# Seven quarter products for eight in the left half of nine down blocks of each feed-forward stage

## The reference

```python
def _swiglu(h, w_gu, w_down):
    g, u = jnp.split(h @ w_gu, 2, axis=-1)
    return (jax.nn.silu(g) * u) @ w_down

x = x + 0.5 * _rmsnorm(_swiglu(_rmsnorm(x, ffn1_pre_g), ffn1_w_gu, ffn1_w_down), ffn1_post_g)
```

## Time and profile before

| | |
|---|---|
| median of 3 runs | 1080.8 us (1080.31 to 1081.05) |
| profiled execution: time | 1081.31 us |
| profiled execution: span, first to last instruction | 1079.4 us |
| mean granted TensorE clock | 1.000 |
| PE busy | 1068.7 us, 99% of the span |
| DVE busy | 789.1 us, 73% |
| ACT busy | 608.5 us, 56% |

### The profile page before, as it was taken

How to read it: one execution, slowest core, us unless ns; L and a number is a source line. 1 busy time by engine, 2 the same in 40 slices (tenths; PEclk the granted TensorE clock), 3 DMA queues, 4 the chain that set the end, 5 groups by cost and what they waited for, 6 DMA issues and landing times.

```text
span 1079.4 us, 21082 instructions
## 1 busy us (share of the span) xinstructions
PE 1068.7 (99%) x8534; PEld 1009.7 (94%) x8534; DVE 789.1 (73%) x1125; ACT 608.5 (56%) x905; POOL 0.2 (0%) x4
## 2 busy tenths in 40 slices
PE   9999999999999999999999999999999999999999
PEld 7999999999989999999999998999999799999898
DVE  5665556989979777778778555775655887997884
ACT  5544444678586545878445556444444575655471
POOL 0000000000000000000000000000000000000000
PEclk9999999999999999999999999999999999999999
DMA  9866556465543454444546533465556355542251
GB/s 343 292 213 211 176 182 209 151 221 174 179 154 121 152 181 157 157 164 149 208 166 244 196 106 130 147 230 198 188 182 212 119 177 200 191 157 95 102 196 39
DMA packets 29297, 190.71 MB, mean 177 GB/s; under 512 B 3656, under 2 KB 4521, under 8 KB 7466
## 3 DMA queue, kind: packets, MB, share of 16 engines
...
HBM read 188.62 MB, written 1.05 MB: 176 GB/s over the span
## 4 chain that ended last, share of the span: by engine, by line
PE 87%; DVE 9%; ACT 2%; issue 1%; DMA 1%; SPq 0%; DVEq 0%; ACTq 0%
PE bank L526 15%; PE bank L528 15%; PE bank L527 15%; PE bank L538 10%; PE bank L539 10%; PE bank L540 10%; DVE sb_w_lo L2098 3%; PE bank L625 2%; PE bank L761 1%; DVE sb_ssd_conv L2409 1%; DMA sb_w_raw<-in_w 1%; PE bank L709 1%; PE bank L886 1%; ACT sb_w_hi L1371 1%; PE bank L1048 1%
## 5 line engine op out<-in xcount | busy, mean ns | idle before, releaser
L2098 DVE TENSOR_TENSOR sb_w_lo<-sb_w_raw,sb_w_hi 128x2048 fp32r<-128x2048 f32 x169 | 386.4, 2289 | 118.9 <-ACT sb_w_hi L1371 118.5
L1371 ACT ACTIVATE sb_w_hi<-sb_w_raw 128x2048 fp32r<-128x2048 f32 x169 | 322.9, 1911 | 33.0 <-PE bank L528 29.2
L526 PE MATMUL bank<-sb_hT_hi,sb_w_hi 128*128 128x256 f32 (+1 forms) x816 | 225.7, 277 | 0.0
L528 PE MATMUL bank<-sb_hT_hi,sb_w_lo 128*128 128x256 f32 (+1 forms) x816 | 225.7, 277 | 0.0
L527 PE MATMUL bank<-sb_hT_lo,sb_w_hi 128*128 128x256 f32 (+1 forms) x816 | 225.6, 276 | 0.0
L538 PE MATMUL bank<-sb_hT_hi,sb_w_hi 128*128 128x256 f32 (+2 forms) x744 | 213.1, 286 | 0.2 <-DVE sb_hT_lo L2175 0.2
L539 PE MATMUL bank<-sb_hT_lo,sb_w_hi 128*128 128x256 f32 (+2 forms) x744 | 206.2, 277 | 0.0
L540 PE MATMUL bank<-sb_hT_hi,sb_w_lo 128*128 128x256 f32 x744 | 205.9, 277 | 0.0
L526 PEld LDWEIGHTS bank<-sb_hT_hi,sb_w_hi 128*128 128x128 f32 (+1 forms) x816 | 152.7, 187 | 0.0
L528 PEld LDWEIGHTS bank<-sb_hT_hi,sb_w_lo 128*128 128x128 f32 (+1 forms) x816 | 152.6, 187 | 0.0
L527 PEld LDWEIGHTS bank<-sb_hT_lo,sb_w_hi 128*128 128x128 f32 (+1 forms) x816 | 152.6, 187 | 0.0
...
## 6 DMA issues: line engine op xcount, KB each, us to landing
sb_w_raw<-in_w SPq DMA_DIRECT2D x169, 1024.0 KB, 4.9
...
```

The costliest lines, as they stand in the source:

```text
L526: pe.matmul(o, a_hi, b_hi, start=first, stop=False)
L528: return pe.matmul(o, a_lo, b_hi, start=False, stop=last)
L1371: act.activation(w_hi[b % STAGES][:], w_raw[b % RING][:], ACT.Copy).then_inc(w_hi_in, 1)
L2098: tt(w_lo[b % STAGES][:], w_raw[b % RING][:], f32(w_hi[b % STAGES][:]), ALU.subtract).then_inc(w_lo_in, 1)
```

## The change

In down blocks 1 to 9 of both stages the left half of the output (512 columns) is computed with seven products of quarters (128 x 128 by 128 x 256) in place of eight, the way of Strassen and Winograd. The pair of hidden tiles by two token halves is one 2 x 2 arrangement, the two row tiles of the weight block by two column quarters the other. The right half is computed as before. A mixed down block thus has 12 matmuls of 512 columns and 21 of 256.

- The host lays the four left quarters of such a block first in the buffer (B11, B12, B22, B21), the right half behind.
- VectorE forms three sums of weight quarters (`mix_block`, three additions on 512, 256 and 256 columns; one replaces B12 in the raw buffer) behind the activation of the even tile, before ScalarE may round the block. ScalarE rounds 768 more columns, VectorE makes 768 more columns of rest.
- VectorE forms four sums of the hidden tiles' halves (128 columns each), one behind the even tile, three inside the odd one; ScalarE rounds them (512 columns), VectorE makes their rest.
- The seven products are collected in banks 5 and 6 and in the left-half banks 3 and 4. Banks 5 and 6 are opened with a product by zeros: bank 6 in stage 1 at the very start of the kernel, the others in down block 0, ahead of its last product. VectorE makes the zero operand `zero_r` ahead of tile 0.
- After down block 9 ScalarE copies two quarters out, VectorE joins four (`join`, four operations of 256 columns): ahead of tile 21 in stage 1, behind tile 21 in stage 2 and ahead of the last `fold_sum`. Behind the stage the joined part is added to banks 0 and 2 (two additions of 512 columns) ahead of the gains, and the squares of these two are taken from the sums.
- The banks of up blocks change (up 2 of stage 1 goes to bank 5), the transposes for the memory's root move from before up 20 to its middle, and down block 10 ends its products in the order 0, 2, 1, 3.

`LAST_DOWN` keeps its values. The diff, cut to its core (the calls `join()` stand ahead of `hidden_tile(FF_TILES - 1, ...)` in stage 1 and behind it in stage 2; `sums_high(1)` stands behind `high(3)` and `sums_high(2, turn)` behind `high(5, turn)` on ScalarE; `part_copies()` behind `after(down_at(n, PAIRS - 2))`):

```diff
+MIXED_OF = {down_at(n, c): MIXED_PAIRS * (n - 1) + c - 1 for n in (1, 2) for c in range(1, PAIRS - 1)}
...
+            def open_mixed(n, q):
+                claim(f"mixed{n}.{q}", 5 + q, down_at(n, PAIRS - 2))
...
+                last_bank = (FIRST[f"ffn{n}"] + 2) % 3
+                down_banks = (3, 7, 4, last_bank)
...
+                    return 5 if n == 1 and j == 2 else (FIRST[f"ffn{n}"] + j % 2) % 3
...
+                def last_product(o, w_hi, w_lo, parts, all_three):
+                    t = slice(P, SEQ)
+                    for m, (a, w) in enumerate(((f["hi"], w_hi), (f["hi"], w_lo), (f["lo"], w_hi))):
+                        at = 0
+                        for width in parts if all_three or m == 2 else (512,):
+                            mm = pe.matmul(o[:, at:at + width], a[:, 1, t], w[:, at:at + width], start=False, stop=False)
+                            at += width
+                    return mm
...
+                def mixed_block(c, turn=0, parts=(512,), all_three=False):
                     b = down_at(n, c)
                     pe.wait_ge(w_lo_in, b + 1 - SPLIT_FROM + TURN * turn)
+                    hi, lo = w_hi[b % STAGES], w_lo[b % STAGES]
+                    top, low = slice(0, P), slice(P, SEQ)
+                    b11, u2, b22, b21 = (slice(MIX_AT + i * 256, MIX_AT + (i + 1) * 256) for i in range(4))
+                    u1, u3, u4 = (slice(i * 256, (i + 1) * 256) for i in range(3))
+                    def plain_half(o, k, t):
+                        h = slice(PLAIN_AT + k * 512, PLAIN_AT + (k + 1) * 512)
+                        return product(o[:], f["hi"][:, k, t], f["lo"][:, k, t], hi[:, h], lo[:, h], False, False)
+                    def of_tile(bank, side, k, t, m_hi, m_lo, m, closes):
+                        product(banks[bank][:, side * 256:(side + 1) * 256], f["hi"][:, k, t], f["lo"][:, k, t],
+                                m_hi[:, m], m_lo[:, m], False, closes and c == PAIRS - 2)
+                    def of_sum(bank, side, i, m_hi, m_lo, m, closes):
+                        product(banks[bank][:, side * 256:(side + 1) * 256], sum_hi[:, i, :], sum_lo[:, i, :],
+                                m_hi[:, m], m_lo[:, m], False, closes and c == PAIRS - 2)
+                    tile_in(c, 0, turn)
+                    plain_half(banks[7], 0, top)
+                    of_tile(5, 0, 0, top, hi, lo, b11, False)
+                    tile_in(c, 1, turn)
+                    plain_half(banks[7], 1, top)
+                    of_tile(3, 0, 1, top, hi, lo, b21, False)
+                    of_tile(4, 0, 1, low, mix_hi, mix_lo, u4, False)
+                    pe.wait_ge(S("ffn_sum_lo"), MIXED_PAIRS * (n - 1) + c + turn)
+                    of_sum(3, 1, 3, hi, lo, b22, False)
+                    of_sum(5, 1, 0, mix_hi, mix_lo, u1, True)
+                    of_sum(6, 0, 1, hi, lo, u2, False)
+                    of_sum(6, 1, 2, mix_hi, mix_lo, u3, True)
+                    plain_half(banks[last_bank], 0, low)
+                    last = slice(PLAIN_AT + 512, PLAIN_AT + 1024)
+                    last_product(banks[last_bank], hi[:, last], lo[:, last], parts, all_three).then_inc(block_done, 1)
...
+                        for i in (0, 2, 1, 3) if last and k else range(4):
+                            o = banks[down_banks[i]]
...
+                            if first and k and i == 3:
+                                pe.wait_ge(S("zero_r"), n)
+                                for q in range(n):
+                                    open_mixed(n, q)
+                                    pe.matmul(banks[5 + q][:], zero_r[:], hi[:, 0, 0:512], start=True, stop=False)
+                                mm = last_product(o, hi[:, 1, h], lo[:, 1, h], parts, all_three)
+                                continue
...
-                down_block(0, 0, *LAST_DOWN[n][0])
+                plain_block(0, *LAST_DOWN[n][0])
                 up_block(3)
                 with pe.Fori(0, PAIR_TURNS) as turn:
                     up_block(4, turn)
-                    down_block(1, turn, *LAST_DOWN[n][1])
+                    mixed_block(1, turn, *LAST_DOWN[n][1])
                     up_block(5, turn)
-                if n == 1:
-                    mem_root_turn()
-                up_block(FF_TILES - 2)
-                down_block(PAIRS - 2, 0, *LAST_DOWN[n][2])
+                up_block(FF_TILES - 2, between=mem_root_turn if n == 1 else None)
+                mixed_block(PAIRS - 2, 0, *LAST_DOWN[n][2])
                 up_block(FF_TILES - 1)
-                down_block(PAIRS - 1)
+                plain_block(PAIRS - 1)
...
+            open_mixed(1, 1)
+            pe.matmul(banks[6][:], zeros[:, 0:P], zeros[:], start=True, stop=False)
...
+                if b in MIXED_OF:
+                    act.wait_ge(S("ffn_mixed"), MIXED_OF[b] + 1 + turn)
+                    act.activation(w_hi[b % STAGES][:], w_raw[b % RING][:], ACT.Copy)
+                    act.activation(mix_hi[:], mix_raw[:], ACT.Copy).then_inc(w_hi_in, 1)
...
+                def sums_high(c, turn=0):
+                    act.wait_ge(S("ffn_sum"), MIXED_PAIRS * (n - 1) + c + turn)
+                    act.activation(sum_hi[:], sum_raw[:], ACT.Copy).then_inc(S("ffn_sum_hi"), 1)
...
+                def part_copies():
+                    o = full(act, f"mixed{n}.0")
+                    act.activation(f["joined"][:, 0, 0:256], o[:, 0:256], ACT.Copy)
+                    copy(f"mixed{n}.0", f["parts"][:, 0, :], o[:, 256:512])
...
+                for m, i in enumerate((0, 2, 1, 3)):
+                    wait_read(act, f"down{n}.{i}")
+                    src = banks[fills[f"down{n}.{i}"][0]][:] if i % 2 else f["joined"][:, i // 2, :]
+                    if m:
+                        act.wait_ge(S("post_ssq"), (0 if n == 1 else POST_SSQ[2]) + m)
+                    act.activation(f["junk"][:], src, ACT.Square, accum_out=post_ssq[:, i // 2, i % 2:i % 2 + 1])\
...
+            def mix_block(b, turn=0):
+                w = w_raw[b % RING]
+                def quarter(first, last):
+                    return w[:, MIX_AT + first * 256:MIX_AT + last * 256]
+                dve.wait_ge(w_landed[b % RING], 16 * (b // RING + 1 + turn))
+                p = MIXED_OF[b]
+                tt(mix_raw[:, 0:512], quarter(0, 2), quarter(1, 3), ALU.add).then_inc(S("ffn_mixing"), 1)
+                dve.wait_ge(S("ffn_mixing"), 2 * p + 1 + 2 * turn)
+                tt(quarter(1, 2), mix_raw[:, 0:256], quarter(2, 3), ALU.add).then_inc(S("ffn_mixing"), 1)
+                dve.wait_ge(S("ffn_mixing"), 2 * p + 2 + 2 * turn)
+                tt(mix_raw[:, 512:768], quarter(1, 2), quarter(3, 4), ALU.add).then_inc(S("ffn_mixed"), 1)
...
+                def first_sum(c, turn):
+                    p = MIXED_PAIRS * (n - 1) + c - 1
+                    even = f["act"][:, 0, :]
+                    if p:
+                        dve.wait_ge(S("ffn_sum_hi"), p + turn)
+                    tt(sum_raw[:, 2, :], even[:, 0:P], even[:, P:SEQ], ALU.subtract).then_inc(S("ffn_summing"), 1)
+                def other_sums(c, turn):
+                    p = MIXED_PAIRS * (n - 1) + c - 1
+                    even, odd = f["act"][:, 0, :], f["act"][:, 1, :]
+                    dve.wait_ge(S("ffn_summing"), 2 * p + 1 + 2 * turn)
+                    tt(sum_raw[:, 1, :], sum_raw[:, 2, :], odd[:, P:SEQ], ALU.add)
+                    tt(sum_raw[:, 0, :], even[:, P:SEQ], odd[:, P:SEQ], ALU.subtract).then_inc(S("ffn_summing"), 1)
+                    dve.wait_ge(S("ffn_summing"), 2 * p + 2 + 2 * turn)
+                    tt(sum_raw[:, 3, :], odd[:, 0:P], sum_raw[:, 1, :], ALU.subtract).then_inc(S("ffn_sum"), 1)
+                def sums_low(c, turn):
+                    p = MIXED_PAIRS * (n - 1) + c - 1
+                    dve.wait_ge(S("ffn_sum_hi"), p + 1 + turn)
+                    tt(sum_lo[:], sum_raw[:], f32(sum_hi[:]), ALU.subtract).then_inc(S("ffn_sum_lo"), 1)
+                def join():
+                    wait_read(dve, f"mixed{n}.0")
+                    y, p5, w = f["joined"], f["parts"][:, 0, :], f["parts"][:, 1, :]
+                    o = full(dve, f"mixed{n}.1")
+                    link(tt(w, o[:, 0:256], y[:, 0, 0:256], ALU.subtract))
+                    link(tt(y[:, 0, 256:512], w, p5, ALU.add))
+                    tt(y[:, 1, 0:256], o[:, 256:512], w, ALU.subtract)
+                    read(tt(y[:, 1, 256:512], y[:, 0, 256:512], o[:, 256:512], ALU.subtract), f"mixed{n}.1")
                 def hidden_tile(j, between, behind, turn=0, ahead_of=()):
...
+                    mixed = 2 <= j < 2 * PAIRS - 2
+                    if mixed:
+                        wait_read(dve, f"up{n}.{j}", turn)
+                        if j % 2:
+                            other_sums(j // 2, turn)
+                    for b in behind:
+                        if b in MIXED_OF:
+                            mix_block(b, turn)
...
```

(20 more changed lines are left out.)

83 lines of the change are left out of this document (51 added, 32 removed).

## The result

| | before | after |
|---|---|---|
| median | 1080.72 us (1080.31 to 1081.05, 4 runs) | 1089.36 us (1089.04 to 1090.16, 4 runs) |
| profiled execution: time, span | 1081.31, 1079.4 us | 1090.16, 1086.7 us |
| PE, DVE, ACT busy | 1068.7, 789.1, 608.5 us | 1067.4, 862.3, 634.9 us |

The changed kernel is slower by 0.8%: ratio 1.0081, 95% interval 1.0064 to 1.0099. A second set of runs of the same kernel gave 1088.6 us and 1.0078 (1.0064 to 1.0092). The forecast was 1086.0 with a range of 1081.5 to 1091.5.

The account below looks back on a forecast made before the run. TensorE's columns were taken to set the time. Stage 1 +4.0, stage 2 +2.8 and the start -1.4 gave +5.4 us, from 1081.31 to 1086.7, adjusted to the median and rounded to 1086.0; range 1081.5 to 1091.5.

Parts of the forecast that it names:

- start, with `zero_r`: Kernel's start: an added fp32 zero product brings the faster clock earlier, -1.4 us; `zero_r` adds 0.2.
- columns, 18 blocks: Mixed down blocks: fewer TensorE columns save 0.21 us a block, 3.8 us over 18 blocks.
- stage 1, last tile: Tile 21 of stage 1: VectorE leaves the loop late and `join` stands ahead, so TensorE waits 2.15 us (1.2 to 2.8).
- kv2, to stage 2 (with up 2): kv2's rest block comes later behind stage 1, wait 0.95 us (0.5 to 1.2); stage 2's up 2 waits 0.1.
- stage 2, up 4 and up 5: Stage 2's first pairs: `mix_block` costs its whole 1.5 us, so each up block waits 0.5 us (0 to 0.9).
- stage 2, last tile: End of stage 2's loop: idle was only 0.18 us, so tile 21's rest makes TensorE wait 1.35 us (0.7 to 2).
- behind stage 2: Behind stage 2: `join`, `fold_sum`, an addition and squares delay the last square; loss 1.8 us (1 to 2).
- the narrow stream stays slow after a mixed block: Rival: up blocks' narrow matmuls run at 0.1178 us, not 0.1135, 6.6 us in 16 turns; 1092 us, chance 0.14.
- The seams do not bind: Rival: VectorE's additions hide wholly, places 2 to 7 (7.5 us) vanish, bank 5's wait stays; 1078.6 us, chance 0.09.
- Nearly level: Rival: narrow matmuls at 0.1135 us (-2.3) and one or two seams smaller; 1079 to 1083 us, chance 0.13.
- A quarter costs a half: Rival: 256-column matmuls are bound by their weight load, so nothing is saved; +20 us or more, chance 0.02.
- Terms 1 and 2: Stage 1: TensorE waits 2.1 us in down block 0 for bank 5's reader, and 0.3 ahead of up 6.

Follow-up runs that it names:

- start_zero: The kernel before with a second fp32 product by zeros at its start, nothing else: 1080.56 us, ratio 1.0002.
- start_filled: The kernel before with a second fp32 zero product at the start and four overwritten products in the wait ahead of stage 1's down block 0: 1081.08 us, ratio 1.0005.
- fill_more: The changed kernel with extra products filling TensorE's waits ahead of and in stage 1's down block 0 and in both down blocks 10: 1087.93 us, ratio 1.0069.
- no_cut: The changed kernel with the last product of the loops' mixed blocks as one matmul of 512 columns, not two of 256: 1094.37 us, ratio 1.0125.
- columns_only: The changed kernel with TensorE's side alone, without the sums, their rounding and rests, and nearly all joining: 1080.64 us, ratio 0.9998.
- open_late: The changed kernel with bank 5 opened by zeros behind up 3 of stage 1, not inside down block 0: 1088.6 us, ratio 1.0075.
- join_behind: The changed kernel with stage 1's joining of quarters behind the last hidden tile instead of ahead of it: 1091.6 us, ratio 1.0101.

## Why the prediction came out as it did

The direction was right, and so was the mechanism: TensorE's columns give 3.3 us, and the additions cost more than that at the seven places at which VectorE had no slack. The size was low: +5.4 forecast, +7.3 between the two profiled spans, +8.1 to +8.6 between the medians. Of the gap between the last two, 0.6 is the profiled execution of the kernel before, which was a slow one of its kind. Term by term, in us, from the two traces:

| step | forecast | measured |
|---|---|---|
| start, with `zero_r` | -1.2 | -0.7 (down block 0 at 26.73; 27.42 before) |
| columns, 18 blocks | -3.8 | -3.3 (0.18 each: 5.30 for 5.48 on the mean) |
| stage 1, down 0, with its zero product | +2.3 | +2.3 (8.07 for 5.74) |
| stage 1, up 6 | +0.3 | +0.5 (up 3 to up 6 without down 1: 22.68 for 22.16) |
| stage 1, last tile | +2.15 | +2.1 (7.59 for 5.51) |
| kv2, to stage 2 (with up 2) | +1.05 | +1.1 (499.82 for 498.69) |
| stage 2, down 0's zero products | +0.45 | +0.45 (5.94 for 5.49) |
| stage 2, up 4 and up 5 | +1.0 | +1.5 (0.74, 0.28 and 0.51) |
| stage 2, last tile | +1.35 | +1.4 (6.94 for 5.51) |
| behind stage 2 | +1.8 | +1.9 (226.35 for 224.47) |

The measured column adds up to 7.3, as it must. The waits were forecast within 0.2 us at each place but up 4 and up 5. Four things failed, and three of them are sizes.

**The start.** "I take -1.4" took the earlier product for an earlier end. The clock did come earlier (first split product at 13.56), but the load of block 3 follows it only in some executions, and start_zero and start_filled show that nothing measurable is left in the median. That is 0.5 us in the profile and more in the medians.

**The pace behind a wait.** In the terms of up 6, up 4 and up 5 ("each 0 to 0.9") a wait was counted at its own length. Behind some waits the narrow matmuls stand 117.8 ns apart and not 113.5, until the next cut product: 47 of them behind the wait at 57.03 (0.2 us), 96 behind the one ahead of up 5 of stage 2 (0.4 us, most of the 0.5 missing there). Without a wait so do the 71 at the start, in up 1 and the first half of up 2 (0.3 us of what the start had gained).

**The columns.** The row taken for the 18 narrow ones (0.1178 each) did not hold for them: they take 0.1194, 2.15 us in all. That is 0.03 us a block, 0.5 in all. The 5.3 us that the prediction worked out from a fixed cost for each matmul are further off than its own 3.8.

**Not foreseen at all: the clock.** The prediction gave the granted clock a part at the start alone. Behind waits of about 2 us it falls in most runs of the changed kernel; the longest wait of the kernel before is 1.84 us, and no run of its 41 reports a fall. fill_more puts the price at about 0.7 us (median span 1086.1, against 1086.8 over the nine runs of the changed kernel), little because VectorE is late there anyway. The Trainium skill describes such a fall (TensorE: Matmul & The Clock Gate, "HAM oscillation — how this bites in real kernels"): a wait between bursts throttles the array again. The runs agree in that, with falls behind waits of 1.8 to 3.2 us and none behind others of the same length.

Of the rivals, "the narrow stream stays slow after a mixed block" would have been true without the cut (no_cut, 5.0 to 5.8 us slower than the changed kernel; forecast 6.6 less 0.8); with it, it holds only behind waits. "The seams do not bind" and "Nearly level" fall with the result itself, and columns_only adds that even with nearly all of the additions gone the time is that of before (1080.6), not 1078.6. "A quarter costs a half" falls with the narrow row, 0.1194 us for 256 columns. Terms 1 and 2, told as two waits, are largely one lateness (open_late).

What stays open: the time outside the span. It is 1.76 to 2.14 us in the 41 runs of the kernel before and 1.8, 1.8, 2.7 and 3.5 in the first four of the changed one, 1.8 to 3.1 in the next five; join_behind has it too (up to 3.5), fill_more and the others do not (1.74 to 2.15). In the first four runs it carries some 0.3 us of the difference of medians, in the next five none, since their median span is itself 8.0 to 8.3 us above that of the kernel before. No run here tells its cause.

No version that computes the whole result beat the kernel before. The best changed one is fill_more, 0.7% slower.
